# Last layer with the weights in the array: memory keys, the cross attention's queries and both attentions' gates made turned, probabilities divided before their turn

## The chip, the cores and the metric

The kernel runs on one core of a Trainium2 chip. The metric is the device time of one execution in microseconds. TensorE (PE) multiplies, ScalarE (ACT) evaluates functions and copies, VectorE (DVE) adds, multiplies and reduces, GpSimd (POOL) and SyncE (SP) mostly issue transfers.

## The reference

256 positions of width 1024 go through three layers. Layers 0 and 1 are an attention mixer (MLA with sliding-window attention; forgetting attention with chunked relative positions) and a SwiGLU. The change is in the last layer and in the memory keys that it reads:

```python
h = rms_norm(x, norm_g[layer])
(qa, ka, va, ga, ub, vb, gb, qc, gc, ma, mb, mc) = split_cols(h @ w_in[layer], IN_SPLITS)
qa = partial_rope(qa.reshape(B, S, MOBA_HEADS, HEAD_DIM_2), pos)
ka = partial_rope(ka.reshape(B, S, MOBA_HEADS, HEAD_DIM_2), pos)
out_a = moba_attention(qa, ka, va) * jax.nn.silu(ga)
out_b = gmlp_spatial_gate(ub, vb, ...) * jax.nn.silu(gb)
mem_n = rms_norm(mem, mem_norm_g[layer])
out_c = memory_cross_attention(qc, mem_n, w_mem_kv[layer]) * jax.nn.silu(gc)
y = (jax.nn.sigmoid(ma) * (out_a @ w_branch_a[layer])
     + jax.nn.sigmoid(mb) * (out_b @ w_branch_b[layer])
     + jax.nn.sigmoid(mc) * (out_c @ w_branch_c[layer]))
x = x + y @ w_out[layer]
```

MoBA has 6 heads of 128 and, at 256 positions, is causal attention over one block. The cross attention has 4 heads of 128 over 256 memory rows. The gMLP has 6 groups of 128.

## The kernel before

**Products.** Every product of weights and activations is made of three passes of 32-bit "r" numbers: both operands are split into a high part (hi) and the rest (lo), and hi x hi, lo x hi and hi x lo are added up. SP loads the weights in chunks of 512 KB, ScalarE casts a chunk to its hi part (L1088), VectorE subtracts to get the lo part (L1401), and TensorE works through the chunks in order. `plan_gemms` lists the products: rows of 128 inputs (k), how many of them a chunk holds, columns of a step, steps. A usual step (`step`, L605, L607, L610) has the activations in the array and 512 columns of weights moving: for each k and each half of the positions three matmuls, 12 for a chunk. The result comes out with positions on the partitions. ScalarE empties a step's two accumulator banks, multiplied by the row's normalisation factor `root`, while the next step uses the other two.

**Blocks.** `step_by_pair` (L992), used for the queries and keys of layer 1, has 128 columns of weights in the array and the activations moving, so that the result comes out turned. For each k and each of the two blocks of 128 columns the hi weights meet hi and lo activations side by side (512 columns, L1009), and the lo weights meet the hi ones (256 columns, L1013). ScalarE copies the half that belongs to the lo activations and VectorE adds the other.

**Last layer.** Its products run in this order: `in_a` (6 steps: MoBA's queries, keys, values, gates), `in_b` and `in_b_end` (4 and a half: gMLP), `in_c` (2: the cross attention's queries and gates), `gate_a`, `branch_a`, `gate_b`, `branch_b`, `gate_c`, `branch_c`, `out`.

**Slots.** The attentions are put between chunks: `between` maps a chunk number to what each engine does after that chunk. A `slot` s of a stream ("moba": heads 0 to 5, "xa": heads 6 to 9 of the count) holds on TensorE, in this order: the turn of query and key of head s (L809), the result product of head s-3 (L822), the turn of the probabilities of head s-2 (L836) and the logits of head s-1 (L849). On VectorE it holds the copy of the turned queries and keys of head s (L1478), result times 1/sum times gate of head s-3 (L1489), the reciprocal of the sum of head s-2 (L1496) and mask, maximum and its negative for head s-1 (L1507, L1511). ScalarE copies the turned probabilities of head s-2 (L1160), casts the chunks that are due, and makes the exponentials of head s-1 (L1169). MoBA's slots follow chunks 2 to 10 of `in_b`, the cross attention's chunks 0 to 6 of `gate_a`; the gates' sigmoid (L1357) shares ScalarE there, with a change of function table either way. The gated results are turned, split and put into `ht_hi`/`ht_lo` by turns "a" (in `in_c`), "b" and "c" (in `branch_a`), L577.

**Order.** The order on each engine is as it is written; an engine waits at semaphores, and what stands behind a wait on the same engine waits with it. `ahead(c)` gives the last chunk to be split by chunk c, from the slots of the weights' buffers.

## Time and profile before

| | us |
|---|---|
| median of three runs | 930.79 |
| lowest, highest | 928.99, 930.91 |
| the profiled execution | 930.03 |
| span of its records | 928.3 |
| TensorE busy | 913.2 (98%) |
| VectorE busy | 582.1 (63%) |
| ScalarE busy | 482.5 (52%) |

The profiled execution's time is 1.7 us more than the span of its records. Busy times of TensorE overlap by a modelled end of each matmul, so distances between two starts tell what a matmul costs, not its duration. A row of a timeline has the start, the duration, engine, line, operation, result <- operands, shape, and the number of instructions that it sums up. A 32-bit matmul of 256 columns stands as two records (x4 for two, x8 for four).

### The profile page before, as it was taken

How to read it: one execution, taken by the hardware profiler on the slowest of the kernel's cores; microseconds unless marked ns; L12 is line 12 of the kernel's file. 1: busy time of each engine (PE TensorE's matmuls, PEld its weight loads, DVE VectorE, ACT ScalarE, POOL GpSimd, SP SyncE). 2: the span in 40 equal slices, each digit the busy share in tenths (PEclk: the TensorE clock that was granted, in tenths of full speed). 3: DMA queues.
4: the chain of work that ended last, by engine and by line, in shares of the span. 5: the costliest groups of instructions: out<-in, count | busy, mean ns of one | idle time of the engine just before them, and what ended most of it. 6: DMA issues, size and time to landing. Idle time of an engine off the chain costs nothing.

```text
span 928.3 us, 12232 instructions
## 1 busy us (share of the span) xinstructions
PE 913.2 (98%) x4534; PEld 755.9 (81%) x4534; DVE 582.1 (63%) x960; ACT 482.5 (52%) x781; POOL 34.4 (4%) x48
## 2 busy tenths in 40 slices
PE   6999999999999999999999999999999999999997
PEld 5887878888888898877888888888888888888875
DVE  4787687555563767768755555476636666574665
ACT  4876564444443456666544444355455654744443
POOL 1100034000000001000000000000000000000000
PEclk9999999999999999999999999999999999999999
DMA  8654467855554568453755556454654465465651
GB/s 301 237 209 136 136 194 205 279 184 190 185 191 157 138 190 257 129 168 135 279 191 182 181 182 210 157 177 151 198 193 138 139 202 159 114 203 182 198 175 58
DMA packets 63145, 169.21 MB, mean 182 GB/s; under 512 B 11016, under 2 KB 25504, under 8 KB 62448
## 3 DMA queue, kind: packets, MB, share of 16 engines
q1 hardware_dynamic: 60448, 156.10, 52.2%
q0 software_dynamic: 2640, 12.35, 4.2%
q8 instruction: 37, 0.61, 0.3%
q14 instruction: 20, 0.16, 0.0%
HBM read 167.36 MB, written 1.06 MB: 181 GB/s over the span
## 4 chain that ended last, share of the span: by engine, by line
PE 96%; DVE 2%; ACT 2%; DMA 1%; issue 0%; SPq 0%; DVEq 0%; ACTq 0%
PE psum L653 21%; PE psum L605 17%; PE psum L610 17%; PE psum L607 17%; PE psum L1009 3%; PE psum L740 3%; PE psum L744 3%; PE psum L750 3%; PE psum L893 2%; PE psum L1013 2%; PE psum L577 1%; PE psum L924 1%; PE psum L907 1%; PE psum L792 1%; PE psum L822 1%; PE psum L849 1%
## 5 line engine op out<-in xcount | busy, mean ns | idle before, releaser
L1401 DVE TENSOR_TENSOR base_lo<-stage,base_hi 128x1024 fp32r<-128x1024 f32 (+3 forms) x223 | 263.3, 1205 | 100.0 <-ACT base_hi L1088 98.9
L1088 ACT CAST base_hi<-stage 128x1024 fp32r<-128x1024 f32 (+3 forms) x223 | 224.4, 1036 | 58.1 <-PE psum L610 32.7
L605 PE MATMUL psum<-base_hi,xt 128*128 128x512 f32 (+3 forms) x464 | 183.5, 395 | 2.6 <-ACT base_hi L1088 2.3
L607 PE MATMUL psum<-base_lo,xt 128*128 128x512 f32 (+3 forms) x464 | 178.3, 384 | 0.4 <-DVE base_lo L1401 0.4
L610 PE MATMUL psum<-base_hi,xt 128*128 128x512 f32 (+3 forms) x464 | 178.6, 385 | 0.0
L1401 DVE TENSOR_TENSOR extra_lo<-stage,extra_hi 128x1024 fp32r<-128x1024 f32 (+1 forms) x68 | 80.4, 1208 | 51.3 <-ACT extra_hi L1088 51.0
L605 PEld LDWEIGHTS psum<-base_hi,xt 128*128 128x128 f32 x464 | 87.7, 189 | 19.4 <-ACT base_hi L1088 2.7
L610 PEld LDWEIGHTS psum<-base_hi,xt 128*128 128x128 f32 x464 | 87.6, 189 | 17.2 <-DVE xt L1441 0.4
L607 PEld LDWEIGHTS psum<-base_lo,xt 128*128 128x128 f32 x464 | 87.7, 189 | 17.1 <-DVE base_lo L1401 1.1
L1088 ACT CAST extra_hi<-stage 128x1024 fp32r<-128x1024 f32 (+1 forms) x68 | 68.4, 1037 | 47.4 <-PE psum L653 26.4
L605 PE MATMUL psum<-extra_hi,xt 128*128 128x512 f32 x160 | 63.2, 395 | 0.0
L610 PE MATMUL psum<-extra_hi,xt 128*128 128x512 f32 x160 | 62.4, 390 | 0.0
L607 PE MATMUL psum<-extra_lo,xt 128*128 128x512 f32 x160 | 62.4, 390 | 0.0
L653 PE MATMUL psum<-base_hi,ht_hi 128*128 128x512 f32 x144 | 51.5, 400 | 0.0
L653 PE MATMUL psum<-base_lo,ht_hi 128*128 128x512 f32 x144 | 50.2, 391 | 0.2 <-DVE base_lo L1401 0.2
L653 PE MATMUL psum<-base_hi,ht_lo 128*128 128x512 f32 x144 | 50.0, 390 | 0.0
L1253 ACT ACTIVATE qk_t<-psum 128x256 f32<-128x256 f32 x44 | 14.5, 382 | 62.0 <-PE psum L610 54.0
L1140 ACT CAST ht_hi<-psum 128x512 fp32r<-128x512 f32 x22 | 12.9, 587 | 63.4 <-PE psum L792 63.4
L1448 DVE TENSOR_TENSOR ht_lo<-psum,ht_hi 128x512 fp32r<-128x512 f32 x22 | 15.2, 691 | 47.4 <-ACT ht_hi L1140 47.3
L605 PE MATMUL psum<-base_hi,ht_hi 128*128 128x512 f32 (+1 forms) x106 | 41.2, 389 | 0.0
L1009 PE MATMUL psum<-xt,base_hi 128*128 128x512 f32 x128 | 41.0, 404 | 0.0
L610 PE MATMUL psum<-base_hi,ht_lo 128*128 128x512 f32 (+1 forms) x106 | 39.4, 372 | 0.0
(202 smaller groups left out, 1407.2 us busy)
## 6 DMA issues: line engine op xcount, KB each, us to landing
stage<-in_w_up SPq DMA_DIRECT2D x80, 512.0 KB, 4.4
stage<-in_w_down SPq DMA_DIRECT2D x44, 512.0 KB, 4.3
stage<-in_w_in_a SPq DMA_DIRECT2D x24, 512.0 KB, 4.7
stage<-in_w_cd_in SPq DMA_DIRECT2D x16, 512.0 KB, 4.8
stage<-in_w_in_b SPq DMA_DIRECT2D x16, 512.0 KB, 4.0
stage<-in_w_ab_in SPq DMA_DIRECT2D x12, 480.0 KB, 6.7
ln_par<-in_ln POOLq DMA_DIRECT2D x4, 1024.0 KB, 7.8
stage<-in_w_ab_out SPq DMA_DIRECT2D x8, 512.0 KB, 3.5
```

The lines of the kernel that those rows point to most:

```text
L605: pe.matmul(acc, ah, wh, start=(k == 0), stop=False)
L607: pe.matmul(acc, ah, wl, start=False, stop=False)
L610: last = pe.matmul(acc, al, wh, start=False, stop=(k == g.kc - 1))
L653: last = pe.matmul(psum[:, 2 * ((g.u0 + half) % 2) + t, :], a, w(c, half * 512, 512), start=(k == 0 and w is w_hi and a is ah), stop=summed)
L740: pe.matmul(acc, ah, w_hi(c, at, g.n), start=(k == 0), stop=False)
L744: pe.matmul(acc, al, w_hi(c, at, g.n), start=False, stop=False)
L750: last = pe.matmul(acc, ah, w_lo(c, at, g.n), start=False, stop=(k == g.kc - 1))
L893: last = pe.matmul(psum[:, LOGIT_BANK + e, t * P:t * P + nk], qk_t[rows, b, t * P:(t + 1) * P], qk_t[rows, b, S:S + nk], start=True, stop= ...
L1009: last = pe.matmul(acc, w_hi(c, at, P), xt[:, k, :, :].rearrange("p a n -> p (a n)"), start=(k == 0), stop=(k == g.kc - 1))
L1013: last = pe.matmul(acc[:, 0:S], w_lo(c, at, P), xt_hi[:, k, :], start=False, stop=False)
L1088: act.copy(w_hi(c, 0, w), stage_of(c, w)).then_inc(hi_done, 1)
L1401: dve.tensor_tensor(w_lo(c, 0, w), stage_of(c, w), w_hi(c, 0, w).bitcast(F32), ALU.subtract).then_inc(lo_done, 1)
```

## The change

- The memory keys are made by blocks, turned, and so are `in_c` (queries and gates of the cross attention) and a new product `in_ga`, which holds MoBA's gates. `in_a` has 5 steps instead of 6, the last with a part of gMLP's columns; `in_b_end` is gone, and its columns are in `in_b`. The arrays of the weights are the same: `in_a`, `in_ga` and `in_b` are read from them as pieces of rows, of 2 KB or 1 KB.
- The cross attention's logits take queries and keys from where they were made; its q/k turns and copies go. Its `root` factor goes into the maximum and the scale of the exponential. MoBA's q/k copy moves from VectorE to ScalarE.
- A gate, turned, is multiplied by the row of root factors on VectorE (`scale_gates`), which GpSimd spreads over the partitions, and goes through SiLU on ScalarE (`make_gates`).
- VectorE divides the probabilities by their sum right after the exponentials, and TensorE waits for that (`head_scaled`) before it turns them. The result product has the values in the array and gives the result turned; VectorE multiplies it by the gate, ScalarE casts it to hi, VectorE makes lo, straight into `ht`. Turns "a" and "c" go; "b" stays.
- MoBA's slots stand two chunks earlier (chunks 0 to 8 of `in_b`), the cross attention's one chunk earlier (slot 1 at chunk 0 of `gate_a`).
- `ht` has hi and lo side by side; SP's wait before the loads of up1 goes.

```diff
-    table = [("ab_in", 8, 2, 480, 3), ("uq", 3, 3, 256, 3), ("ukv", 2, 2, 512, 2), ("mem_k", 8, 2, 512, 1),
+    table = [("ab_in", 8, 2, 480, 3), ("uq", 3, 3, 256, 3), ("ukv", 2, 2, 512, 2), ("mem_k", 8, 4, 256, 2),
              ("mem_v", 8, 2, 512, 1), ("ab_out", 8, 1, 1024, 1), ("up0", 8, 2, 512, 11), ("down0", 22, 1, 1024, 1),
              ("cd_v", 8, 2, CD_V // 3, 3), ("cd_qk", 8, 4, 256, 8), ("cd_out", 8, 1, 1024, 1), ("up1", 8, 2, 512, 11), ("down1", 22, 1, 1024, 1),
-             ("in_a", 8, 2, 512, 6), ("in_b", 8, 2, 512, 4), ("in_b_end", 8, 4, 256, 1), ("in_c", 8, 2, 512, 2),
+             ("in_a", 8, 2, 512, 5), ("in_ga", 8, 4, 256, 3), ("in_b", 8, 2, 512, 4), ("in_c", 8, 4, 256, 4),
...
+AB_COLUMNS = [(0, 3 * AW, "in_a", 0), (3 * AW, 2048, "in_b", 0), (3 * AW + 2048, 3 * BW - 2048, "in_b_end", 0)]
...
+    if g.name == "in_ga":
+        return [(0, g.n, "in_a", 3 * AW + j * g.n)]
+    if g.name in ("in_a", "in_b"):
+        j += 0 if g.name == "in_a" else PRODUCTS["in_a"].steps
+        return runs(AB_COLUMNS, j * g.n, (j + 1) * g.n)
...
-                    dv = hd.v(0).shape[-1]
-                    for t in range(TT):
-                        kts = range(TT) if hd.full or t else range(1)
-                        for kt in kts:
-                            n = (kt * TT + t) if hd.full else (t + kt)
-                            last = pe.matmul(psum[:, O_BANK, t * dv:(t + 1) * dv],
-                                             probs_t[:, h % 2, n * P:(n + 1) * P], hd.v(kt),
-                                             start=(kt == 0), stop=(kt == kts[-1]))
+                    for kt in range(TT):
+                        first = 0 if hd.full else kt * P
+                        last = pe.matmul(psum[:, O_BANK, first:S], hd.v(kt),
+                                         probs_t[:, h % 2, kt * S:kt * S + S - first], start=(kt == 0), stop=(kt == 1))
                     last.then_inc(pv_ready, 1)
                 h = lo_h + s - 2
                 if lo_h <= h < hi_h:
                     hd = head_of(2 * PAIRS + h)
-                    pe.wait_ge(exp_ready, h + 1)
+                    pe.wait_ge(head_scaled, h + 1)
...
+                        q, k = qk_t[:, h % 2, 0:S], qk_t[:, h % 2, S:2 * S]
+                    else:
+                        q, k = hd.q, hd.k
...
-            gemm("mem_k", ht_hi, ht_lo, 0, None, attending("mem_k", *range(4)))
+            blocks("mem_k", ht, attending("mem_k", *range(4)))
...
+            blocks("in_ga", xt)
+            gemm("in_b", xt_hi, xt_lo, 0, None, {0: moba_first, **{s: slots("moba", s) for s in range(1, 9)}})
...
-            gemm("in_c", xt_hi, xt_lo, 0, None,
-                 {0: lambda: turn("a", tile_of(a2), [(head_done, 6)], [0]),
-                  1: lambda: turn("a", tile_of(a2), [(head_done, 6)], [1]),
-                  **{2 + g: lambda g=g: mix([g]) for g in range(6)}})
+            blocks("in_c", xt, {2 + g: lambda g=g: mix([g]) for g in range(6)})
 
             def xa_first():
+                pe.wait_ge(*read("mem_k", 2))
                 pe.wait_ge(*read("in_c", 2))
-                heads_banks("b")
                 pe.wait_ge(gated_b, 6)
-                slot("xa", 0)
-
-            gemm("gate_a", xt_hi, xt_lo, 0, None, {0: xa_first, **{s: slots("xa", s) for s in range(1, 7)}})
-            gemm("branch_a", ht_hi, ht_lo, 0, "a",
-                 {0: lambda: turn("b", tile_of(b2), [(gated_b, 6), (head_done, 10)], [0]),
-                  1: lambda: turn("b", tile_of(b2), [], [1]),
-                  2: lambda: turn("c", tile_of(c2), [(head_done, 10)])})
+                slot("xa", 1)
+
+            gemm("gate_a", xt_hi, xt_lo, 0, None, {0: xa_first, **{s: slots("xa", s + 1) for s in range(1, 6)}})
+            pe.wait_ge(gated_hi, MOBA_H)
+            pe.wait_ge(gated_lo, MOBA_H)
+            gemm("branch_a", ht_hi, ht_lo, 0, None,
+                 {0: lambda: turn("b", tile_of(b2), [(gated_b, 6), (max_ready, 10)], [0]),
+                  1: lambda: turn("b", tile_of(b2), [], [1])})
...
+                h = lo_h + s - 4
+                if lo_h <= h < hi_h:
+                    act.wait_ge(head_done, h + 1)
+                    act.copy(ht_hi[:, gated_at(h), :], head_of(2 * PAIRS + h).gate).then_inc(gated_hi, 1)
+                h = lo_h + s
+                if stream == "moba" and h < hi_h:
+                    act.wait_ge(qk_turned, h + 1)
+                    if h >= 2:
+                        act.wait_ge(logits_ready, h - 1)
+                    act.copy(qk_t[:, h % 2, :], psum[:, QK_BANK, :]).then_inc(qk_copied, 1)
...
+                                              scale=root(t) if hd.full else 1.0, accum_out=soft[:, b, 2, t:t + 1])
                     last.then_inc(exp_ready, 1)
+
+            def copy_block_lows(name, j):
+
+
+                count, u, dst, highs, lows = block_sums(name, j)
+                act.wait_ge(chunk_used, PRODUCTS[name].c0 + 2 * j + 2)
+                act.copy(dst, lows).then_inc(block_lows, 1)
+
+            def make_gates(name, j, count):
+                dst = block_sums(name, j)[2]
+                act.wait_ge(gate_scaled, count)
+                act.activation(dst, dst, ACT.Silu).then_inc(gate_ready, 1)
...
+            act.preload_act_table(ACT.Silu)
+            gemm("in_ga", None, {1: lambda: copy_block_lows("in_ga", 0), 2: lambda: make_gates("in_ga", 0, 1),
+                                 3: lambda: copy_block_lows("in_ga", 1), 4: lambda: make_gates("in_ga", 1, 2),
+                                 5: lambda: copy_block_lows("in_ga", 2)})
+
+            def last_gates():
+                make_gates("in_ga", 2, 3)
+                act.preload_act_table(ACT.Exp)
+                slot("moba", 0)
+
+            gemm("in_b", columns_from(2560), {0: last_gates, **{s: slots("moba", s) for s in range(1, 10)},
...
+            def xa_first():
+                make_gates("in_c", 3, 5)
+                slot("xa", 1)
+
+            gemm("gate_a", gate, {0: xa_first, **{s: slots("xa", s + 1) for s in range(1, 7)}})
...
-                        dve.wait_ge(logits_ready, h - 1)
-                    dve.tensor_copy(qk_t[:, h % 2, :], psum[:, QK_BANK, :]).then_inc(qk_copied, 1)
+                    dve.wait_ge(gated_hi, h + 1)
+                    at = gated_at(h)
+                    dve.tensor_tensor(ht_lo[:, at, :], head_of(2 * PAIRS + h).gate, ht_hi[:, at, :].bitcast(F32),
+                                      ALU.subtract).then_inc(gated_lo, 1)
                 h = lo_h + s - 3
                 if lo_h <= h < hi_h:
                     hd = head_of(2 * PAIRS + h)
+                    dve.wait_ge(gate_ready, gates_made(h))
                     dve.wait_ge(pv_ready, h + 1)
-                    dv = hd.v(0).shape[-1]
-                    for t in range(TT):
-                        o, r = psum[:, O_BANK, t * dv:(t + 1) * dv], soft[:, h % 4, 4, t:t + 1]
-                        if hd.gate is None:
-                            last = dve.tensor_scalar(hd.out(t), o, r, None, ALU.mult)
-                        else:
-                            last = dve.scalar_tensor_tensor(hd.out(t), o, r, hd.gate(t), ALU.mult, ALU.mult)
-                    last.then_inc(head_done, 1)
-                h = lo_h + s - 2
-                if lo_h <= h < hi_h:
-                    hd = head_of(2 * PAIRS + h)
-                    b = h % 4
-                    dve.wait_ge(exp_ready, h + 1)
-                    settle(dve.reciprocal(soft[:, b, 4, :], soft[:, b, 2, :]))
+                    dve.tensor_tensor(hd.gate, psum[:, O_BANK, 0:S], hd.gate, ALU.mult).then_inc(head_done, 1)
...
+                if hd.full:
+                    dve.scalar_tensor_tensor(soft[:, b, 1, :], soft[:, b, 0, :], -1.0, rms_st[:, 3, 2, :],
+                                             ALU.mult, ALU.mult).then_inc(max_ready, 1)
+                else:
                     dve.tensor_scalar(soft[:, b, 1, :], soft[:, b, 0, :], -1.0, None, ALU.mult).then_inc(max_ready, 1)
+                split_to(done["due"])
+                dve.wait_ge(exp_ready, h + 1)
+                settle(dve.reciprocal(soft[:, b, 4, :], soft[:, b, 2, :]))
+                for t in range(TT):
+                    part = probs[:, h % 2, t * n0:t * n0 + (S if t else n0)]
+                    last = dve.tensor_scalar(part, part, soft[:, b, 4, t:t + 1], None, ALU.mult)
+                last.then_inc(head_scaled, 1)
+
+            def add_block_lows(name, j):
+                count, u, dst, highs, lows = block_sums(name, j)
+                dve.wait_ge(block_lows, count)
+                dve.tensor_tensor(dst, dst, highs, ALU.add).then_inc(acc_free[u % 2], TT)
+
+            def scale_gates(name, j):
+
+                add_block_lows(name, j)
+                count, u, dst, highs, lows = block_sums(name, j)
+                dve.wait_ge(acc_free[u % 2], TT * (u // 2 + 1))
+                dve.wait_ge(root_spread, 16)
+                dve.tensor_tensor(dst, dst, view(root_row, 0, [[0, 2], [1, S]]), ALU.mult).then_inc(gate_scaled, 1)
...
+            gemm("in_c", None, {1: lambda: add_block_lows("in_c", 0), 2: lambda: gate_b([0]),
+                                3: lambda: [add_block_lows("in_c", 1), gate_b([1])], 4: lambda: gate_b([2]),
+                                5: lambda: [scale_gates("in_c", 2), gate_b([3])], 6: lambda: gate_b([4]),
+                                7: lambda: [scale_gates("in_c", 3), gate_b([5])]})
+            gemm("gate_a", None, {s: slots("xa", s + 1) for s in range(7)})
```

On TensorE, the slot after chunk 4 of `gate_a` (L822 is the result product, L836 the turn of probabilities, L849 the logits), before:

```order
L607 MATMUL psum<-base_lo,xt 128x512
L610 MATMUL psum<-base_hi,xt 128x512
L822 MATMUL psum<-arena,probs_t 128x128 x4
L836 MATMUL psum<-ident,pair_probs 128x128 x4
L849 MATMUL psum<-qk_t 128x256 x2
L605 MATMUL psum<-base_hi,xt 128x512
```

and the slot after the same chunk, after (L895 is the result product, L908 the turn; L651, L653 and L656 are the lines of a step):

```order
L653 MATMUL psum<-base_lo,xt 128x512
L656 MATMUL psum<-base_hi,xt 128x512
L895 MATMUL psum<-probs_t,arena 128x256 x2
L908 MATMUL psum<-ident,pair_probs 128x128 x4
L651 MATMUL psum<-base_hi,xt 128x512
L653 MATMUL psum<-base_lo,xt 128x512
L656 MATMUL psum<-base_hi,xt 128x512
```

Everything of a cross head has moved one chunk up: before, head 2's probabilities were turned here and head 3's logits made; now it is head 3's turn, and the logits were made at chunk 3.

On ScalarE, around the evacuation of the first step of `gate_a` (L1357 and `ln_par` are the gate's sigmoid, L1088 the hi cast of a chunk), before:

```order
L1169 ACTIVATE pair_probs,soft<-pair_probs,soft 128x256 x2
L1357 ACT_TABLE_LOAD
L1357 ACTIVATE ln_par<-psum,rms_st 128x512 x2
L1160 COPY probs_t<-psum 128x512
L1088 CAST base_hi<-stage 128x1024
L1169 ACT_TABLE_LOAD
L1169 ACTIVATE pair_probs,soft<-pair_probs,soft 128x256 x2
```

and after:

```order
L1228 ACTIVATE pair_probs,soft<-pair_probs,soft,rms_st 128x256 x2
L1445 ACT_TABLE_LOAD
L1445 ACTIVATE ln_par<-psum,rms_st 128x512 x2
L1205 CAST ht<-arena 128x256
L1219 COPY probs_t<-psum 128x512
L1137 CAST base_hi<-stage 128x1024
L1228 ACT_TABLE_LOAD
L1228 ACTIVATE pair_probs,soft<-pair_probs,soft,rms_st 128x256 x2
```

The cast of a gated result (L1205) has come in between the evacuation and the next exponentials.

On VectorE, one slot in the middle of the cross attention, before:

```order
L1478 COPY qk_t<-psum 128x512
L1489 SCALAR_TENSOR_TENSOR arena<-psum,soft,arena 128x128 x2
L1496 RECIPROCAL soft<-soft 128x2
L1507 ISA pair_probs,soft<-psum,no_mask 128x256
L1507 ISA soft 128x1
L1507 ISA pair_probs,soft<-psum,no_mask 128x256
L1507 ISA soft 128x1
L1511 TENSOR_SCALAR soft<-soft 128x2
L1401 TENSOR_TENSOR base_lo<-stage,base_hi 128x1024
```

and after:

```order
L1569 TENSOR_TENSOR ht<-arena,ht 128x256
L1576 TENSOR_TENSOR arena<-psum,arena 128x256
L1588 ISA pair_probs,soft<-psum,no_mask 128x256
L1588 ISA soft 128x1
L1588 ISA pair_probs,soft<-psum,no_mask 128x256
L1588 ISA soft 128x1
L1593 SCALAR_TENSOR_TENSOR soft<-soft,rms_st 128x2
L1492 TENSOR_TENSOR base_lo<-stage,base_hi 128x1024
L1599 RECIPROCAL soft<-soft 128x2
L1602 TENSOR_SCALAR pair_probs<-pair_probs,soft 128x256 x2
```

The copy is gone, the split of the chunk (L1401, now L1492) stands ahead of the reciprocal, and the two scalings of the probabilities follow it.

## Rows read from the trace of the kernel before

**Rows 1.** The page's chain that ended last; busy times from 643 to 911 us.
```profile
PE 96%; DVE 2%; ACT 2%; DMA 1%; issue 0%; SPq 0%; DVEq 0%; ACTq 0%
...
core 0: us, PE busy (x) PEld busy (x) DVE busy (x) ACT busy (x) POOL busy (x), PEclk, DMA share, GB/s
643.00:911.00 268.00, 267.80 (x1302) 224.11 (x1301) 160.46 (x247) 141.05 (x199) 0.53 (x1) 1.00 0.54 172
```

**Rows 2.** Timeline of TensorE in a chunk of gate_a (start us, duration us).
```profile
793.12 0.39 PE L610 MATMUL psum<-base_hi,xt 128*128 128x512 f32 x1
...
795.17 0.40 PE L610 MATMUL psum<-base_hi,xt 128*128 128x512 f32 x1
```

**Rows 3.** Timeline of TensorE, the two parts of turn "a" in in_c.
```profile
752.17 0.82 PE L577 MATMUL psum<-ident,arena 128*128 128x128 f32 x6
...
755.58 0.82 PE L577 MATMUL psum<-ident,arena 128*128 128x128 f32 x6
```

**Rows 4.** Timeline of TensorE, slots after chunks 2 to 4 of gate_a.
```profile
786.38 1.03 PE L849 MATMUL psum<-qk_t 128*128 128x256 f32 x4
...
790.02 0.60 PE L809 MATMUL psum<-ident,arena 128*128 128x128 f32 x4
790.46 1.06 PE L822 MATMUL psum<-arena,probs_t 128*128 128x128 f32 x8
791.35 0.60 PE L836 MATMUL psum<-ident,pair_probs 128*128 128x128 f32 x4
...
796.30 0.60 PE L836 MATMUL psum<-ident,pair_probs 128*128 128x128 f32 x4
```

**Rows 5.** Timeline of TensorE, a step by blocks of layer 1.
```profile
365.00 0.63 PE L1009 MATMUL psum<-xt,base_hi 128*128 128x512 f32 x2
...
366.39 0.63 PE L1009 MATMUL psum<-xt,base_hi 128*128 128x512 f32 x2
```

**Rows 6.** Timeline of TensorE, first matmul of in_b_end and first of in_c.
```profile
743.67 0.28 PE L605 MATMUL psum<-base_hi,xt 128*128 128x256 f32 x1
...
749.42 0.40 PE L605 MATMUL psum<-base_hi,xt 128*128 128x512 f32 x1
```

**Rows 7.** Groups by form (count | busy us, mean ns of one | idle before).
```profile
L1560 DVE TENSOR_SCALAR pair_probs<-pair_probs,pair_st 128x256 f32<-128x256 f32 x32 | 11.1, 348 | 0.0
...
L1496 DVE RECIPROCAL soft<-soft 128x2 f32<-128x2 f32 x10 | 1.5, 155 | 0.0
...
L1196 ACT CAST ht_hi<-psum 128x256 fp32r<-128x256 f32 x8 | 3.0, 372 | 13.1 <-PE psum L924 13.1
...
L1311 ACT COPY qk_t<-psum 128x512 f32<-128x512 f32 x8 | 4.5, 568 | 2.9 <-PE psum L1009 2.9
...
L1401 DVE TENSOR_TENSOR base_lo<-stage,base_hi 128x1024 fp32r<-128x1024 f32 x200 | 240.1, 1225 | 92.0 <-ACT base_hi L1088 91.3
```

**Rows 8.** Timeline of ScalarE in gate_a.
```profile
789.46 0.19 ACT L1169 ACTIVATION_READ_ACCUMULATOR pair_probs<-pair_probs,soft 128x1 f32 x1
...
793.67 1.28 ACT L1169 ACT_TABLE_LOAD   x1
794.96 0.51 ACT L1169 ACTIVATE pair_probs<-pair_probs,soft 128x256 f32<-128x256 f32 x1
...
795.87 0.19 ACT L1169 ACTIVATION_READ_ACCUMULATOR pair_probs<-pair_probs,soft 128x1 f32 x1
```

**Rows 9.** Timeline of ScalarE and TensorE, MoBA heads 0 and 2.
```profile
701.69 0.19 ACT L1169 ACTIVATION_READ_ACCUMULATOR pair_probs<-pair_probs,soft 128x1 f32 x1
...
702.90 0.49 PE L836 MATMUL psum<-ident,pair_probs 128*128 128x128 f32 x3
...
710.72 0.19 ACT L1169 ACTIVATION_READ_ACCUMULATOR pair_probs<-pair_probs,soft 128x1 f32 x1
...
712.61 0.49 PE L836 MATMUL psum<-ident,pair_probs 128*128 128x128 f32 x3
```

**Rows 10.** The page's DMA issues (count, KB each, median us to landing).
```profile
stage<-in_w_in_a SPq DMA_DIRECT2D x24, 512.0 KB, 4.7
stage<-in_w_cd_in SPq DMA_DIRECT2D x16, 512.0 KB, 4.8
```

More of the change, by code:

```diff
@@ L1349, in _, with columns_from, evacuate @@
-            gemm("in_a", pieces(a2, 3 * AW))
-            act.preload_act_table(ACT.Exp)
-            gemm("in_b", pieces(b2, 2 * BW), {**{2 + s: slots("moba", s) for s in range(9)},
-                                              14: lambda: [deviation(4, 0, 1), deviation(4, 1, 1)]})
-            gemm("in_b_end", lambda j, t, acc: pieces(b2, 2 * BW)(4, t, acc, 256))
-            gemm("in_c", pieces(c2, CW), {0: lambda: turn("a", ht_hi, 0, [0]), 1: lambda: turn("a", ht_hi, 0, [1])})
+            def columns_from(first):
+                def evacuate(j, t, acc):
+                    lo = first + j * 512
+                    cuts = [lo, *[m for m in (3 * AW, 3 * AW + 2 * BW) if lo < m < lo + 512], lo + 512]
+                    for at, end in zip(cuts, cuts[1:]):
+                        dst = a2[:, t, at:end] if at < 3 * AW else b2[:, t, at - 3 * AW:end - 3 * AW]
+                        last = act.activation(dst, acc[:, at - lo:end - lo],
+                                              ACT.Silu if at >= 3 * AW + 2 * BW else ACT.Copy, scale=root(t))
+                        if end < lo + 512:
+                            settle(last)
+                    return last
+                return evacuate
@@ L1813, in _ @@
             gemm("in_a", None, {13: moba_positions})
+            gemm("in_ga", None, {2 * j + 1: lambda j=j: scale_gates("in_ga", j) for j in range(3)})
             def gmlp_stats():
@@ L1829, in gmlp_norm @@
                 last.then_inc(vn_ready, 1)
[L1831 to L1832 removed]
+            gemm("in_b", None, {**{s: slots("moba", s) for s in range(1, 10)}, 13: gmlp_stats, 15: gmlp_norm})
             def gate_b(groups):
[L1836 removed]
+                dve.wait_ge(*read("in_b", 4))
                 for g in groups:
```

254 lines of the change are left out of this document (137 added, 117 removed).

## The prediction

> **What bounds the kernel now.** I read the page first, for its chain of work that ended last, and then the busy time in the stretch of the last layer. The chain is TensorE for 96% of the span [rows 1], and from 643 to 911 us TensorE idles for 0.2 of 268 us at a granted clock of 1.00, its higher level, while VectorE is busy for 60% of that time and ScalarE for 53% [rows 1]. So a product or a turn that leaves TensorE's instruction order is worth its whole length there, and work on the other two engines costs nothing until one of them is late for a wait of TensorE. The question is where the change makes them late. The third reading is therefore the order of time around the slots of the cross attention, where the margin before each wait can be taken off.
>
> **The unit.** Between two rows of L610 that stand nine products of 512 columns apart lie 2.05 us, 0.228 us for one [rows 2]. A chunk of twelve takes 2.73 us, and 256 output columns cost three of them, 0.683 us, for each k.
>
> **What leaves TensorE.** Turn "a": two blocks of 12 products with six transposes each stand 3.41 us apart, 0.68 more than a chunk [rows 3], and there are two: 1.36 us. Turn "c" is eight transposes, by the same rows 0.68 x 8/6 = 0.91 us. The queries' and keys' turns of four cross heads: 790.02 to 790.46 is 0.44 us [rows 4], four times 1.76 us. The result product: 790.46 to 791.35, 0.89 us for a cross head [rows 4]; with the value in the array it streams as many columns by two wider instructions, so nothing to 0.15 us is saved over ten heads; I take nothing. Together 4.03 us leave.
>
> **What the block form adds.** Memory keys, the gates of MoBA, and queries and gates of the cross attention are 9 steps of 256 columns in the form that the fox layer has at L1009 and L1013. There the products of two k take 1.39 us [rows 5], 0.695 each, against 0.683 before, for as many streamed columns. 72 times 0.012 is 0.9 us; the rounding of the starts makes it 0.5 to 1.3. The step in_b_end goes: its 48 products of 256 columns took 749.42 - 743.67 = 5.75 us [rows 6], and as part of full steps the same columns take 8 x 0.683 = 5.47, so 0.3 comes off. Net +0.6 us.
>
> **What is hidden.** Emptying a block step is one ScalarE copy of 0.57 us (L1311 [rows 7]) and one VectorE add of the same tile inside the 5.5 us of the next step, as in the fox layer. Scaling the gates is a further VectorE pass of about the same length, and the SiLU calls lie ahead of result products that come three slots later. The q/k copy of MoBA moves from VectorE to ScalarE at 0.57 us; ScalarE has 47% of the stretch free. The row of root factors goes over GpSimd's queue before final_g, which only the end of the kernel reads, and gpsimd is idle. SP loses its wait before up1, which I put at nothing. If any of that cover failed, it would be through the waits that follow.
>
> **The wait that the division adds.** Before, TensorE turned a head's probabilities as soon as ScalarE had the exponentials, and 1/sum was put in at the result. Now the turn waits for VectorE too: a reciprocal (155 ns) and two scalings (348 ns each) [rows 7], with the steps between them about 0.9 us after the last exponential. Behind that wait on TensorE stand the logits of the next head and all later chunks. Three margins:
> First, cross head 3, now turned at chunk 4 of gate_a, where head 2 was. ScalarE's queue there holds the gate's two evacuations, a copy, a cast, a change of table and then the exponentials. They ended at 795.87 + 0.19 = 796.06, and TensorE came to the turn at 796.30: 0.24 us to spare [rows 4, 8]. After: TensorE is 0.44 earlier (one turn less between this head's logits and there), ScalarE has one cast of a gated result more, 0.37 alone and some 0.3 in a queue [rows 7], and the division adds 0.9. The wait is 0.44 + 0.3 + 0.9 - 0.24 = 1.4 us. Its bounds are 0.9, if the cast falls in ScalarE's idle time and the gap closes elsewhere, and 1.8.
> Second, cross head 0, turned at chunk 1 with no result product ahead. From the start of a head's logits, 786.38 + 1.03, to its last exponential, 789.46 + 0.19, are 2.24 us [rows 4, 8]; with the division 3.1, against the 2.7 us of a chunk: a wait of about 0.5 (0 to 1.8, if the table load, 1.28 us [rows 8], falls in the middle).
> Third, MoBA. The exponentials of head 2 ended at 710.72 + 0.19 = 710.91 and its turn began at 712.61 [rows 9]: 1.70 us, 0.8 with the division. For head 0, which has no result product ahead of its turn and an evacuation ahead of its exponentials, the same rows give 702.90 - 701.88 = 1.02, so 0.1 is left. The other slots lie between these two; where an evacuation stands in them I put 0.35, an estimate. I take no wait, with 0 to 0.5. A last 0.1 is for the wait on the gated gMLP groups, which now come right behind a shorter in_c. Together +2.0 us.
>
> **The sum.** -4.0 + 0.6 + 2.0 = -1.4 us. Against the profiled run's own 930.03 us that is **928.6 us**. The median of the three runs is 930.79, 0.8 above the profiled run, and they spread over 1.9; so the sum is smaller than what single runs differ by. The bound for a difference that can be told from none is 0.2%, 1.9 us: faster is below 928.2, slower above 931.9.
>
> **A rule against the change.** Each table load stands 1.29 us before its next instruction, 793.67 to 794.96, so nothing follows the load but the work [rows 8]. The Trainium skill, "ScalarE: Activation LUTs", section "What ACT_TABLE_LOAD costs", gives 1283 ns for the load and 1380 ns more for a drain with every switch. The load agrees, while the trace shows no drain behind it; by that rule there would be 2 x 1.4 us more in the queue of head 3.
>
> **The rivals.**
> *The waits don't appear.* ScalarE could run through its queue earlier than I take it, since it has less to do in in_c, and the logits come a chunk sooner relative to the evacuation. Then -4.0 + 0.6 = -3.4, 926.6 us. For it: all margins now are positive. Against it: head 3's is only 0.24 us, and over 1 us is put into it.
> *The lo split falls on the path of the division (slower).* VectorE works through the split of the due chunks (1.2 us each, L1401 [rows 7]) before it waits for the exponentials. The split needs ScalarE's hi cast, and ScalarE now has the 0.57 us copy and the 0.3 us cast of a gated result ahead of it in a MoBA slot. If the split ends after the exponentials by its whole length, the wait is 1.2 - 0.8 = 0.4 us in three MoBA heads, and 1.2 - 0.35 = 0.85 in the three beside an evacuation: 3.8 us, -1.4 + 3.8 = +2.4, 932.4 us. It decides from the point where ScalarE's casts lie over 0.8 us later in the slot. Against it: the cast is anchored to TensorE's use of a buffer a chunk back, and the two engines are idle for over 40% of the time.
> *The loads come late.* in_a, in_b and in_ga are read as pieces of rows, of 2 KB and 1 KB, instead of whole contiguous chunks. The fox layer's pieces of 1 KB land after 4.8 us, contiguous chunks of in_a after 4.7 [rows 10], so no difference shows. If the pieces that straddle two arrays did each cost one chunk's landing once, 4.7 us, the time would be 933.3.
> *A switch of tables costs more than the load.* If 1.3 us followed each of two switches, as long again as the load, head 3 would wait 2.6 us more: +1.2, 931.2 us. Rows 8 speak against it. The drain of the Trainium skill's page would make it 2.8 and 931.4.
> *Loads of the array show.* The block form loads the array four times for each k, the step three times. If TensorE could not load beneath a product, the extra load were visible. A product of 512 columns is started every 0.228 us [rows 2] and one of 256 columns every 5.75/48 = 0.12 us [rows 6], each with a load of its own, so hardly anything of a load shows. If the 0.11 us of one transpose (0.44 for four, above) were the price of a load, 72 x 0.11 = 7.9 us would come on top: 936.5 us. The Trainium skill, "TensorE: Matmul & The Clock Gate", section "The mechanism", says that a load overlaps matmuls in flight only when the row groups differ, which they don't here. By it this rival would hold; the spacing of the trace speaks against it.
>
> **How the numbers follow.** The forecast, its waits within their bounds: 0.54 (its own range 927.6 to 929.6; 0.08 faster, 0.45 same, 0.01 slower). No waits: 0.22 (0.20 faster, 0.02 same). The split on the path: 0.13 (0.11 slower, 0.02 same). Late loads 0.06, slower. Tables 0.04 (0.02 same, 0.02 slower). Loads of the array 0.01, slower. Faster 0.28, same 0.51, slower 0.21. The range takes in the case without waits, with 0.5 us for the spread of runs, and reaches up to the split's 932.4: 926.1 to 932.4. Beyond it are the late loads, the array and the tails, under 0.2.
>
> **What would show it.** In the profile after: TensorE's waits list a line for the turn of probabilities, released by VectorE's scaling, with one wait of 1 to 2 us in gate_a and one of about 0.5, and hardly any in in_b; block products at 0.70 us a k in mem_k, in_ga and in_c; a chunk of in_c without turns at 2.7 to 2.8 us. Wrong would be: no such line (first rival), or six or more entries in in_b, with VectorE's split ending after ScalarE's exponentials (second), or TensorE waiting for ScalarE's cast while the DMA queue is what it waits for (third).

## The result

The changed kernel takes 938.33 us (median of 4 runs, 938.00 to 939.86) against 930.21 for the kernel before, a ratio of 1.0089 with a 95% interval of 1.0077 to 1.0101. It is 8.1 us slower where 928.6, a gain of 1.4 us, had been forecast. The profiled run has a span of 936.1 us. The page of the changed kernel, its busy times and its chain of work that ended last (compare [rows 1]):

```profile
span 936.1 us, 12249 instructions
...
PE 913.1 (98%) x4518; PEld 754.8 (81%) x4518; DVE 589.2 (63%) x978; ACT 491.0 (52%) x798; POOL 35.7 (4%) x50
...
PE 88%; DVE 4%; ACT 4%; DMA 2%; issue 1%; SPq 0%; DVEq 0%; ACTq 0%
```

TensorE is as busy as before, 913.1 against 913.2 us, but the chain that was TensorE's for 96% is so for 88%: DVE, ACT and DMA have taken the place. What TensorE waited for (us in total, times, longest):

```profile
PE psum L651 <- ACT base_hi L1137: 7.1, 2, 5.6
PE psum L623 <- DMA ident<-in_ident: 4.8, 1, 4.8
PE psum L908 <- DVE pair_probs L1602: 2.1, 2, 1.6
PE psum L653 <- DVE base_lo L1492: 0.8, 2, 0.4
```

The third line is the forecast one: two waits for the divided probabilities, 1.6 and 0.5 us. The first line holds a wait of 5.6 us that the sum had not. The kernel before had a single wait on such a cast, at the start of the program:

```profile
PE psum L605 <- ACT base_hi L1088: 2.3, 1, 2.3
```

The timeline of the changed kernel around its wait of 5.6 us (start, duration, engine, line, result <- operands, and in brackets the idle time ahead and who ended it):

```profile
643.50 0.61 PE L796 MATMUL psum<-base_lo,xt 128*128 128x512 f32 x2
644.70 0.57 POOL L604 DMA_DIRECT2D arena<-root_dram  x1 [8.57 <-DMA root_dram<-rms_st]
648.49 1.04 ACT L1137 CAST base_hi<-stage 128x1024 fp32r<-128x1024 f32 x1 [10.26 <-DMA stage<-in_w_in_a]
...
649.68 0.77 PE L651 MATMUL psum<-base_hi,xt 128*128 128x512 f32 x1 [5.56 <-ACT base_hi L1137]
...
650.85 0.80 PE L653 MATMUL psum<-base_lo,xt 128*128 128x512 f32 x1 [0.40 <-DVE base_lo L1492]
651.44 0.63 PE L656 MATMUL psum<-base_hi,xt 128*128 128x512 f32 x1
651.87 0.63 PE L651 MATMUL psum<-base_hi,xt 128*128 128x512 f32 x1
```

Read upwards: TensorE waits for ScalarE's cast of in_a's ninth chunk, the first of its third step (the expectations below call it the fifth, which is not so: the fifth to eighth were staged in time), ScalarE has idled 10.26 us for the DMA of that chunk, and in the same stretch GpSimd has waited 8.57 us for its own small store, the 1 KB of root factors on the way to DRAM. From the last product ahead to the third behind it, three starts take 7.0 us more than three spacings. Then products start every 0.43 us instead of 0.228 for seven spacings more, 1.4 us: TensorE had stood still, and the granted clock was down, 0.83 on average from 640 to 660 us, where the kernel before had 1.00. That is 1.2 GHz, the lower of the clock's two levels, until about 654. The same window before and after:

```profile
640.00:660.00 20.00, 20.00 (x90) 16.53 (x89) 10.25 (x10) 11.09 (x13) 0.00 (x0) 1.00 0.72 232
...
640.00:660.00 20.00, 14.04 (x53) 10.79 (x52) 6.76 (x6) 7.25 (x8) 0.57 (x1) 0.83 0.75 224
```

(The columns are those of [rows 1].) So one place costs 8.4 us, and the five steps of in_a take 64.83 us where they took 56.25 before. The transfers in 635 to 650 us, of the changed kernel (40 slices: busy tenths and GB/s; then issues with KB each and us to landing):

```profile
DMA  0000109999003020640190764332212899999999
GB/s 0 0 0 0 3 0 66 49 82 5 0 0 16 0 87 16 27 16 16 5 55 22 33 11 22 22 11 11 16 22 93 257 333 371 382 399 421 404 377 339
...
stage<-in_w_in_a SPq DMA_DIRECT2D x4, 512.0 KB, 12.7
arena<-root_dram POOLq DMA_DIRECT2D x1, 128.0 KB, 6.4
root_dram<-rms_st POOLq DMA_DIRECT2D x1, 1.0 KB, 9.0
```

For some nine microseconds hardly anything moves, and then 250 to 420 GB/s. The four chunks that wait there land after 12.2 to 13.1 us; the four at the same place in the kernel before landed after 3.6 to 5.3. The store of 1 KB has itself taken 9.0 us. Two things of the change meet here: the chunks of in_a come as pieces of rows, and the store is in flight ahead of them. The runs had to tell these apart.

### The profile page after: what moved, and what is told of

The parts are those of the page before. It is cut to its first block, busy times and chain, and to the rows that moved or that the text cites. A ratio compares the mean times of both kernels' runs of the same rounds, so it can differ in the third digit from the quotient of the medians.

```text
span 936.1 us, 12249 instructions
## 1 busy us (share of the span) xinstructions
PE 913.1 (98%) x4518; PEld 754.8 (81%) x4518; DVE 589.2 (63%) x978; ACT 491.0 (52%) x798; POOL 35.7 (4%) x50
## 4 chain that ended last, share of the span: by engine, by line
PE 88%; DVE 4%; ACT 4%; DMA 2%; issue 1%; SPq 0%; DVEq 0%; ACTq 0%
PE psum L699 19%; PE psum L653 15%; PE psum L656 15%; PE psum L651 15%; PE psum L866 6%; PE psum L871 3%; PE psum L786 3%; PE psum L790 2%; PE psum L796 2%; PE psum L968 1%; PE psum L623 1%; DMA stage<-in_w_in_a 1%; PE psum L999 1%; DVE base_lo L1492 1%; PE psum L838 1%
## 5 line engine op out<-in xcount | busy, mean ns | idle before, releaser
L1492 DVE TENSOR_TENSOR base_lo<-stage,base_hi 128x1024 fp32r<-128x1024 f32 (+3 forms) x223 | 264.0, 1206 | 106.9 <-ACT base_hi L1137 105.8
L651 PE MATMUL psum<-base_hi,xt 128*128 128x512 f32 (+2 forms) x400 | 160.0, 400 | 7.5 <-ACT base_hi L1137 7.1
L653 PE MATMUL psum<-base_lo,xt 128*128 128x512 f32 (+2 forms) x400 | 155.9, 390 | 0.8 <-DVE base_lo L1492 0.8
L656 PE MATMUL psum<-base_hi,xt 128*128 128x512 f32 (+2 forms) x400 | 156.0, 390 | 0.0
L1492 DVE TENSOR_TENSOR extra_lo<-stage,extra_hi 128x1024 fp32r<-128x1024 f32 (+1 forms) x68 | 80.3, 1206 | 49.7 <-ACT extra_hi L1137 49.3
L651 PEld LDWEIGHTS psum<-base_hi,xt 128*128 128x128 f32 x400 | 76.2, 190 | 23.0 <-issue 6.9
L653 PEld LDWEIGHTS psum<-base_lo,xt 128*128 128x128 f32 x400 | 76.1, 190 | 16.4 <-DVE base_lo L1492 2.0
L656 PEld LDWEIGHTS psum<-base_hi,xt 128*128 128x128 f32 x400 | 75.9, 190 | 15.3 <-DVE xt L1533 0.4
L699 PE MATMUL psum<-base_hi,ht 128*128 128x512 f32 x288 | 87.6, 395 | 0.0
L866 PE MATMUL psum<-xt,base_hi 128*128 128x512 f32 x240 | 76.5, 403 | 0.0
L699 PEld LDWEIGHTS psum<-base_hi,ht 128*128 128x128 f32 x288 | 53.5, 188 | 12.3 <-DVE pair_probs L1782 0.6
L651 PE MATMUL psum<-extra_hi,xt 128*128 128x512 f32 x160 | 63.2, 395 | 0.0
L656 PE MATMUL psum<-extra_hi,xt 128*128 128x512 f32 x160 | 62.4, 390 | 0.0
L653 PE MATMUL psum<-extra_lo,xt 128*128 128x512 f32 x160 | 62.3, 390 | 0.0
L699 PE MATMUL psum<-base_lo,ht 128*128 128x512 f32 x144 | 50.2, 391 | 0.1
L871 PEld LDWEIGHTS psum<-xt,base_lo 128*128 128x128 f32 x240 | 42.9, 188 | 9.2
L1540 DVE TENSOR_TENSOR ht<-psum,ht 128x512 fp32r<-128x512 f32 x22 | 15.2, 692 | 48.2 <-ACT ht L1189 48.0
L871 PE MATMUL psum<-xt,base_lo 128*128 128x256 f32 x240 | 45.0, 279 | 0.0
```

The lines of the kernel that those rows point to most:

```text
L651: pe.matmul(acc, ah, wh, start=(k == 0), stop=False)
L653: pe.matmul(acc, ah, wl, start=False, stop=False)
L656: last = pe.matmul(acc, al, wh, start=False, stop=(k == g.kc - 1))
L699: last = pe.matmul(psum[:, 2 * ((g.u0 + half) % 2) + t, :], a, w(c, half * 512, 512), start=(k == 0 and w is w_hi and a is ah), stop=summed)
L866: last = pe.matmul(acc, w_hi(c, at, P), joint[:, k, :, :].rearrange("p a n -> p (a n)"), start=(k == 0), stop=(k == g.kc - 1))
L871: last = pe.matmul(acc[:, 0:S], w_lo(c, at, P), joint[:, k, 0, :], start=False, stop=False)
```

## The experiments

**Theory S:** the store of the root factors holds up the loads issued behind it. **Rival P:** the row pieces are slow there and the store is harmless. **Rival C:** it takes both. Each run comes with runs of the kernel before on the same chip, 930.2 to 930.8 us.

**The store alone, in the kernel before.**

```diff
 (GpSimd's queue of before)
             load("gmlp_g", row_g[:, 0:BW], row(d["gmlp_g"], BW))
+            pool.wait_ge(rms_done, 8)
+            pool.dma_start(bass.AP(tensor=root_dram.tensor, offset=0, ap=[[1, P], [P, TT]]), rms_st[:, 3, 2, :],
+                           allow_slow_non_contiguous=True).then_inc(root_stored, 16)
+            pool.wait_ge(root_stored, 16)
```

> The kernel before with one thing more: GpSimd stores the 256 root factors (1 KB, in elements of 4 bytes) to DRAM at the place where the changed kernel does, right behind the last normalisation; nothing reads them. Its loads of in_a are whole chunks. Theory S (the store holds up the loads of weights that are issued behind it): in_a's first loads in the base buffers land after some 13 us instead of 4.7, TensorE waits about 6 to 8 us for the cast of in_a's fifth chunk, about 8 us slower than before, 938. Rival P (the loads as pieces of rows are late, the store is harmless): no difference to before, 930 within 1 us. Rival C (both are needed): no difference either, and then e2 gains.

Measured: 939.37 us, ratio 1.0096 (1.0081 to 1.0111). Nothing reads what is stored, the weights come in whole chunks, and the loss is there, in full. TensorE's waits, the store, and the landings of the four loads behind it (shortest, median, longest):

```profile
PE psum L611 <- ACT base_hi L1094: 8.0, 2, 5.8
...
root_dram<-rms_st POOLq DMA_DIRECT2D x1, 1.0 KB, 11.1
...
DMA to landing us min/median/max: 12.4/12.7/12.8
```

**The changed kernel without row pieces for in_a and in_ga.**

```diff
-                for at, width, array, column in pieces:
+                for at, width, array, column in (() if g.name in ("in_a", "in_ga") else pieces):
...
+                if g.name in ("in_a", "in_ga"):
+                    m = (c - PRODUCTS["in_a"].c0) % 24
+                    sp.dma_start(stage_of(c, WIDTH[c]), bass.AP(tensor=d["w_in_a"].tensor, offset=m * P * 1024,
+                                                               ap=[[1024, P], [1, 1024]])).then_inc(...)
...
```

> The changed kernel with in_a and in_ga loaded as whole contiguous chunks of 512 KB in one transfer each (in rows of 4 KB) instead of pieces of rows; the columns are then not the right ones, so what MoBA computes is not the reference's. The store of the root factors stays. Theory S: the wait of 5 to 6 us at the fifth chunk of in_a stays, the time is the changed kernel's 938 within 1 us. Rival P or C: the wait goes, and with it the time at the low clock, together some 8 us: 930.

Measured: 939.68 us, ratio 1.0096 (1.0079 to 1.0113), the wait 6.3 us:

```profile
PE psum L656 <- ACT base_hi L1142: 8.0, 2, 6.3
```

Rivals P and C fall: without the row pieces nothing is gained back, and the store by itself, without the rest of the change, costs as much as the whole change did.

**The store later, and the store in elements of 8 bytes.**

```diff
             pool.wait_ge(rms_done, 8)
+            pool.wait_ge(chunk_used, PRODUCTS["in_a"].c0 + 8)
```

> The changed kernel with the store held back until TensorE has used eight chunks of in_a (a wait on GpSimd alone). Theory S: the loads that are issued then have more time before they are needed, so that most of the 8.4 us (a wait of 5.7, 1.3 us in the two products behind it and 1.4 us of products at the low clock) goes: 929.5 to 931. What is left against before is then -4.0 + 0.6 + the waits for the divided probabilities, measured 2.4: -1.0 us. Rival P: 938, unchanged.

```diff
-            pool.dma_start(bass.AP(tensor=root_dram.tensor, offset=0, ap=[[1, P], [P, TT]]), rms_st[:, 3, 2, :],
+            pool.dma_start(bass.AP(tensor=root_dram.tensor, offset=0, ap=[[TT, P], [1, TT]]), rms_st[:, 3, 2, :],
...
-                dve.tensor_tensor(dst, dst, view(root_row, 0, [[0, 2], [1, S]]), ALU.mult).then_inc(gate_scaled, 1)
+                dst = dst.rearrange("p a (t n) -> p a t n", t=TT)
+                dve.tensor_tensor(dst, dst, view(root_row, 0, [[0, 2], [1, TT], [TT, P]]), ALU.mult).then_inc(...)
```

> The changed kernel with the store in 128 elements of 8 bytes (both tiles' factors of a position side by side) instead of 256 of 4 bytes; VectorE reads the spread row with a stride. Same bytes, half the elements. Theory S, with a cost by element: the store takes some 5 instead of 9 us, the loads behind it are late by half as much, 4 us less: 933 to 935. With a cost by store: 938. Rival P: 938.

Measured: 931.77 us (1.0019, 1.0009 to 1.0028) and 931.60 (1.0013, 1.0004 to 1.0022). Neither came where it was expected. The later store still took 9.1 us and held three loads behind it to 9.6 to 10.0 us; they had more lead, so a wait of 1.0 us was left of it, and the time missed 929.5 to 931 by 0.8. The 8-byte store landed after 4.0 us and gained more than half; its loads landed after 7.0 to 8.1 us, and two waits were left, 0.3 and 0.7 us. What TensorE waited for, first with the later store, then with the 8-byte one (the longest wait of L651, 2.3 us, is the one at the start of the program):

```profile
PE psum L654 <- DVE base_lo L1493: 1.4, 2, 1.0
...
PE psum L651 <- ACT base_hi L1137: 2.6, 2, 2.3
PE psum L653 <- DVE base_lo L1492: 1.1, 2, 0.7
```

Either way 6.6 to 6.7 us of the medians are back.

**Both at once.** The edit is the sum of the two.

> The changed kernel with both edits of the store at once: held back until eight chunks of in_a are used, and in 128 elements of 8 bytes. Either alone left TensorE a wait for a load of 1 to 2.5 us. Theory S: none is left, and the rest of the change shows alone: the last layer 1.0 us shorter than in the kernel before, ratio 0.9985 to 0.9995 (some 929.8 against 930.8). If the difference that is left came from something else that the change brings (the row pieces, the casts), the time stays at e3's and e4's 931.7.

Measured: 929.41 us against 930.20, ratio 0.9998 (0.9989 to 1.0007). Of TensorE's waits in the last layer, those for the probabilities are left, and none of the others is over 0.2 us:

```profile
PE psum L909 <- DVE pair_probs L1603: 2.1, 2, 1.6
```

The ratio was expected at 0.9985 to 0.9995, its estimate is just outside, the interval covers both. So the times alone do not show a gain. The traces, of one execution each, tell it finer. The program's first product starts to differ by chance: the second one, uq, began at 49.3 us in the kernel before and between 48.9 and 50.6 in the thirteen other profiles, the code up to there being the same. From the last product with weights in the extra buffers, which are in_a's first chunks, to the last matmul, practically the last layer, the kernel before takes 285.61 us and f1 284.47, 1.14 less. The changed kernel takes 293.13, so that the store alone is worth 8.7.

**The wait for cross head 3.** ScalarE's evacuation of the gate's first step moved behind the last exponentials.

```diff
-            gemm("gate_a", gate, {0: xa_first, **{s: slots("xa", s + 1) for s in range(1, 7)}})
+            def gate_out(j):
+                g = PRODUCTS["gate_a"]
+                pair = (g.u0 + j) % 2
+                act.wait_ge(chunk_used, g.c0 + 4 * j + 4)
+                for t in range(TT):
+                    gate(j, t, psum[:, 2 * pair + t, :]).then_inc(acc_free[pair], 1)
+
+            def last_turned():
+                slot("xa", 5)
+                gate_out(0)
+
+            gemm("gate_a", None, {0: xa_first, **{s: slots("xa", s + 1) for s in range(1, 7)}, 4: last_turned,
+                                  7: lambda: gate_out(1)})
```

> f1, and ScalarE empties gate_a's first step (two sigmoids of 1.26 us, with a change of table before and behind) only after the last head's exponentials, one chunk later. Theory Q (the wait of 1.77 us before the turn of cross head 3 comes from that stretch of ScalarE's queue, with the division on top): TensorE's wait for head 3 is gone, 1.7 us less than f1, 928.1 against before's 930.8; the wait for head 0 (0.6 us) stays. Rival D (the wait is the division's on VectorE): some 0.9 us of the wait stay.

Measured: 928.46 us, ratio 0.9984 (0.9975 to 0.9993), 0.95 us less than f1 in the medians; in the traces gate_a's chunks take 31.91 us instead of 33.71, and the last layer is 1.73 us shorter, as forecast. Nothing stays of head 3's wait, so the rival that the division by itself makes it falls. One wait is left, head 0's:

```profile
PE psum L909 <- DVE pair_probs L1615: 0.5, 1, 0.5
```

The wait came from ScalarE's queue. In the changed kernel's trace the chain can be read off:

```profile
799.35 1.28 ACT L1445 ACT_TABLE_LOAD   x1
...
800.64 1.27 ACT L1445 ACTIVATE ln_par<-psum,rms_st 128x512 f32<-128x512 f32 x2
...
801.80 0.40 ACT L1205 CAST ht<-arena 128x256 fp32r<-128x256 f32 x1
802.09 0.60 ACT L1219 COPY probs_t<-psum 128x512 f32<-128x512 f32 x1
...
802.57 1.06 ACT L1137 CAST base_hi<-stage 128x1024 fp32r<-128x1024 f32 x1
...
803.65 1.28 ACT L1228 ACT_TABLE_LOAD   x1
...
804.95 0.60 ACT L1228 ACTIVATE pair_probs<-pair_probs,soft,rms_st 128x256 f32<-128x256 f32 x1
...
806.26 0.17 DVE L1599 RECIPROCAL soft<-soft 128x2 f32<-128x2 f32 x1 [1.25 <-ACT pair_probs L1228]
806.46 0.62 DVE L1602 TENSOR_SCALAR pair_probs<-pair_probs,soft 128x256 f32<-128x256 f32 x2
...
807.13 0.66 PE L908 MATMUL psum<-ident,pair_probs 128*128 128x128 f32 x4 [1.60 <-DVE pair_probs L1602]
```

ScalarE has no gap from 799.35 to 806.23, and VectorE's division, 806.26 to 807.08, is the last 0.9 us before the turn.

**Logits ahead of the turn.** In a cross slot TensorE now makes the next head's logits before it turns the last one's probabilities.

```diff
...
+                for part in ((logits, turned) if stream == "xa" else (turned, logits)):
+                    part()
```

> f2, and TensorE makes the next cross head's logits (0.43 us) before it turns the last one's probabilities, in every cross slot. Theory: the wait of 0.62 us for head 0 falls to 0.2 us, as the logits fill it; 0.4 us less than f2. If logits that come earlier take VectorE from the division, the wait stays at 0.6 and others appear.

Measured: 927.62 us, ratio **0.9975** (0.9965 to 0.9984), gate_a 31.43 us, 0.48 less, and no wait on the probabilities over 0.2 us in the list. This version is the fastest one, 2.6 us below the kernel before's median in that comparison.

**No division at all.** This kernel is f1 again, without f2's and f3's edits, and leaves the softmax's normalisation in the last layer out.

```diff
-                    pe.wait_ge(head_scaled, h + 1)
+                    pe.wait_ge(exp_ready, h + 1)
...
-                dve.wait_ge(exp_ready, h + 1)
-                settle(dve.reciprocal(soft[:, b, 4, :], soft[:, b, 2, :]))
-                for t in range(TT):
-                    part = probs[:, h % 2, t * n0:t * n0 + (S if t else n0)]
-                    last = dve.tensor_scalar(part, part, soft[:, b, 4, t:t + 1], None, ALU.mult)
-                last.then_inc(head_scaled, 1)
```

> f1 without the division: VectorE makes neither the reciprocal nor the scalings, and TensorE turns the exponentials as they are, waiting for ScalarE alone (this leaves the normalisation of the last layer's attentions out). It prices the division where it stands. By the sum of the prediction 0.9 us of head 3's wait and all of head 0's are the division's: TensorE's waits in gate_a fall from 2.4 to 0.9 us, 1.5 us less than f1. If the queue of ScalarE is the whole of head 3's wait (1.77 us stays), only 0.6 is gained.

Measured: 928.69 us, ratio 0.9982 (0.9973 to 0.9990); gate_a takes 32.12 us against f1's 33.71, 1.59 less where 1.5 was expected (the medians differ by 0.7), and what stays is ScalarE's:

```profile
PE psum L909 <- ACT pair_probs L1229: 0.7, 1, 0.7
```

**What of the store is slow.** Four variants of e1's store, each in the kernel before; only the pattern differs.

```diff
 128 of 4 byte:    ap=[[1, P], [P, 1]],         rms_st[:, 3, 2, 0:1]
 128 of 8 byte:    ap=[[TT, P], [1, TT]],       rms_st[:, 3, 2, :]
 128 of 512 byte:  ap=[[P, P], [1, P]],         ident[:, :]
 256, 64 B apart:  ap=[[16, P], [16 * P, TT]],  rms_st[:, 3, 2, :]
```

> e1 with half of the store: 128 elements of 4 bytes (one tile's factors), next to each other in DRAM. If the cost goes by the number of elements, the delay of the loads is halved and most of it fits into their lead: as in e4, 0.5 to 2 us slower than before. If it goes by the element's size or by neighbours in DRAM, it stays at 5 us or more.

> e1 with the same 1 KB in 128 elements of 8 bytes, as e4 has it in the changed kernel. By number of elements: the same as g1, 0.5 to 2 us slower than before. It tells whether e4's gain belongs to the store alone.

> e1 with a store of 64 KB in 128 elements of 512 bytes (the identity matrix) in place of the factors. If bytes mattered, this would be 64 times e1. By number of elements: like g1 and g2, at most 2 us slower. If small elements alone are slow to write: no difference to before, within 1 us.

> e1's 256 elements of 4 bytes, but 64 bytes apart in DRAM instead of next to each other. If the elements delay each other since neighbours are written into the same place of the memory, the delay falls to under 3 us. If it is the number of elements: 8 to 9 us slower than before, as e1.

| store | landing us | the four loads behind it, us | time us | ratio (95%) | last layer against before, us |
|---|---|---|---|---|---|
| none (before) | | 3.6 to 5.3 | | | 285.61 |
| 256 x 4 B, adjacent (e1) | 11.1 | 12.4 to 12.8 | 939.37 | 1.0096 (1.0081 to 1.0111) | +9.3 |
| 128 x 4 B, adjacent | 8.7 | 10.5 to 11.0 | 938.56 | 1.0084 (1.0069 to 1.0099) | +6.6 |
| 128 x 8 B, adjacent | 4.2 | 5.9 to 7.5 | 931.55 | 1.0011 (1.0002 to 1.0021) | +0.5 |
| 128 x 512 B | 1.8 | 3.6 to 5.0 | 930.12 | 0.9994 (0.9985 to 1.0004) | 0.0 |
| 256 x 4 B, 64 B apart | 2.1 | 3.8 to 5.5 | 930.81 | 1.0001 (0.9992 to 1.0011) | -0.1 |

The time is a median, the last column comes from the one profiled execution, measured as for f1 (e1's was the slowest of its four, that of 128 x 4 B the fastest). The landings of the stores are in the traces' list of DMA issues, shown here

```profile
root_dram<-rms_st POOLq DMA_DIRECT2D x1, 0.5 KB, 8.7
...
root_dram<-rms_st POOLq DMA_DIRECT2D x1, 1.0 KB, 4.2
...
root_dram<-rms_st POOLq DMA_DIRECT2D x1, 1.0 KB, 2.1
```

for the 128 x 4 B, the 128 x 8 B and the spaced variant. The expectation that cost goes by the number of elements alone, on which e4's had been built too, is wrong: 128 adjacent elements of 4 bytes cost far more than half of what 256 do, the same number with 8 bytes each holds the loads up by some 2 us only, and 256 spaced ones cost nothing that shows. So in these variants the loss needs elements next to each other in DRAM, and wider ones lessen it. Not shown is whether the width itself counts or how many elements share a stretch of DRAM, nor how far apart is enough: 64 bytes is the only spacing that was run.

## Why the prediction was wrong

**The step that failed** is one sentence in "What is hidden": the row of root factors goes over GpSimd's queue, which is idle. The queue was idle, and the wait for the row cost no engine anything. But the transfer was priced at nothing by looking only at who waits for its result and at how full its queue was. What it does to the transfers around it was not asked, and it was issued at 635.40, 0.9 us ahead of the first loads into base buffers that in_a waits for (636.26), whose cast has to be under way some 6.5 us later. It cost 8.4 us. Nothing in the trace before shows such a store. The one other store in the middle of the kernel, the forgetting attention's rows at 338.1 us, writes 8 KB in rows of 1 KB and lands after 4.4 us, while the core's transfers go on at 200 to 410 GB/s from half a microsecond after it; with its wide elements it tells nothing of a store in elements of 4 bytes. The waits in the sum were given bounds on both sides, and this transfer got none.

**The rival "the loads come late"** had the symptom right (TensorE waits for ScalarE's cast while the DMA is what it waits for), named a time of 933.3, and had the wrong cause: the row pieces. Rows 10 spoke against them rightly, as e2 shows. Its chance of 0.06 was worked out for that cause alone, and a rival for the store was missing.

**The rest of the sum**, with the store out of the way (f1), by the stretches of the last layer in the traces:

| term | forecast | measured |
|---|---|---|
| turn "c" gone (branch_a 18.59 to 17.69) | -0.91 | -0.90 |
| gates of MoBA by blocks (in_ga 16.76, 24 k) | +0.3 | +0.4 |
| memory keys by blocks (18.20 to 18.60, 16 k) | +0.2 | +0.4 |
| in_b, MoBA's waits (56.44 to 56.42) | 0 | 0.0 |
| in_b_end's columns in full steps (what is left of the last layer's -1.14) | -0.3 | -0.3 |
| in_c without turn "a", by blocks (25.84 to 24.70) | -1.0 | -1.1 |
| gate_a: q/k turns gone, waits added (32.82 to 33.71) | +0.2 | +0.9 |
| of this, wait for head 3 | 1.4 | 1.76 |
| of this, wait for head 0 | 0.5 | 0.62 |

(Forecasts for in_ga and in_c are 24 and 32 k at 0.012 us; in_c's has turn "a" with -1.36. The two waits are starts of the turns later than TensorE's spacing gives, and lie within gate_a.) With memory keys the change is worth -0.7 us once the store is out of the way, where -1.4 was forecast: the waits were 0.4 us longer than taken, the block form 0.1 dearer, and the start of the logits 0.25 us slower behind a chunk, without a turn ahead of it, which no row had shown. With some 8.6 us for the store, less 0.7, this is the 7.8 us by which the changed kernel's span is longer (936.1 against 928.3).

**Head 3's wait** was the right mechanism, 1.76 against a bound of 1.8. ScalarE's queue and the division stand one behind the other in it: with the evacuation out of the queue nothing is left (f2), and without the division 0.7 us is (f4), so that 0.9 to 1.1 of it is the division, where 0.9 was taken. The rival of a second 1.3 us behind a table load is refuted again: 803.65 + 1.28 and the exponential starts at 804.95. The Trainium skill, "ScalarE: Activation LUTs", section "What ACT_TABLE_LOAD costs", adds 1380 ns of drain to a switch; the trace agrees with its 1283 ns for the load and shows no drain in this queue.

**The lo split on the path of the division** did not come: in_b is as long as before. **Waits that don't appear** did not come either. **Loads of the array** don't show: in_ga takes 16.76/24 = 0.698 us a k, where that rival asked for some 0.8.

**The range**, 926.1 to 932.4, was made of the priced cases. The time of 938.3 lay outside all of them.

## What to carry to other kernels

A transfer that nobody waits for is not free: ask what is queued behind it on the DMA engines and how much lead that has, above all at a place where an engine has just freed its buffers. A small scattered store belongs where loads have lead, and its elements 64 bytes apart, or, if they are adjacent, as wide as can be. When a step that ends a softmax is moved ahead of another engine's wait, look first at what else stands in the queue that feeds it: one evacuation moved by a chunk gave back more (1.8 us in gate_a) than the division cost there (1.6).

## What the runs showed of the hardware

- A store of 1 KB from 128 partitions, in 256 neighbouring elements of 4 bytes, lands after 11.1 us and holds the four loads of 512 KB behind it, which SP's queue issues, to 12.4 to 12.8 us; with half the elements it is 8.7 and 10.5 to 11.0. The same 256 elements 64 bytes apart land after 2.1 us, and the loads after 3.8 to 5.5, against 3.6 to 5.3 without a store. In the changed kernel the transfers of the whole core moved mostly 10 to 50 GB/s meanwhile, then some 400. Which part of the path does it is not shown. The Trainium skill, "DMA: Bandwidth & Descriptors", section "Specifications", gives 512 bytes as the smallest transfer for full rate and says that SDMA reads, modifies and writes below it. The store of 512-byte elements, landed after 1.8 us, agrees. By that sentence alone the spaced store would be no better than the adjacent one; the measurement, 2.1 against 11.1 us, decides: here the neighbourhood of the elements counts.
- A halt of 5.6 us of TensorE was followed by 1.4 us lost at the clock's lower level, and one of 3.9 us (128 x 4 B) by six starts 0.43 us apart again; the halt of 1.6 us in gate_a was not followed by any.
- The memory keys' blocks took 0.025 us a k more than the step form, MoBA's gates 0.016, layer 1's 0.012 by [rows 5].
